# Three raw weight buffers, weight combinations made later, and an activation stash read straight into the operand

## The reference

```python
def swiglu(h, w1, w3, w2):
    return (jax.nn.silu(h @ w1) * (h @ w3)) @ w2
...
    x = x + 0.5 * swiglu(rmsnorm(x, ffn1_norm[l]), ffn1_w1[l], ffn1_w3[l], ffn1_w2[l])
    h = rmsnorm(x, mix_norm[l])
    proj = h @ w_in[l]                                   # (B,S,IN_W)
    ...
    o = jnp.concatenate([o_fox, o_moba, o_mem], axis=1)  # (B,16,S,Dh)
    ...
    x = x + o @ w_out[l]
    x = x + 0.5 * swiglu(rmsnorm(x, ffn2_norm[l]), ffn2_w1[l], ffn2_w3[l], ffn2_w2[l])
```

## Time and profile before

| | |
|---|---|
| runs | 4636.07, 4637.81, 4639.07 us |
| the profiled execution | 4634.58 us; its slowest core's span 4633.0 us |
| spans of cores 0 to 7 | 4633.0, 4618.8, 4598.5, 4592.8, 4629.0, 4617.3, 4626.0, 4613.5 us |
| TensorE (PE) busy, core 0 | 4378.5 us, 95% |
| VectorE (DVE), ScalarE (ACT) | 3280.9 us, 71%; 1508.3 us, 33% |
| DMA queues | software (GpSimd's) 43.0%, hardware (SyncE's) 26.3% of 16 engines |
| granted TensorE clock | 0.990 on average |

### The profile page before, as it was taken

The page is one execution under the profiler, slowest core; times in us unless marked ns, Lnnn a source line. Parts: engine busy times, 40 slices in busy tenths (PEclk is TensorE's granted clock), DMA queues, the critical chain, the costliest instruction groups (busy, mean ns, idle before and its releaser), DMA issues.

```text
span 4633.0 us, 66912 instructions; the slowest of 8 cores (4592.8 to 4633.0 us)
## 1 busy us (share of the span) xinstructions
PE 4378.5 (95%) x20213; PEld 1992.2 (43%) x20624; DVE 3280.9 (71%) x5577; ACT 1508.3 (33%) x2688; POOL 199.2 (4%) x357
## 2 busy tenths in 40 slices
PE   6998999999999998989999999799999999999999
PEld 2443444444444443444444444344444444444444
DVE  6675778766767876765566777667777887767776
ACT  2323212123121223556559872132221212122121
POOL 0000000000000000000010000000000000000000
PEclk9999999999999999999999999899999999999999
DMA  5788698876949887523357537877869785776845
GB/s 143 118 189 185 136 205 189 194 176 139 206 89 201 198 178 192 140 59 83 78 133 142 120 99 217 211 165 150 168 122 212 176 240 115 157 155 121 195 92 182
DMA packets 229027, 726.35 MB, mean 157 GB/s; under 512 B 25584, under 2 KB 53336, under 8 KB 186176
## 3 DMA queue, kind: packets, MB, share of 16 engines
q0 software_dynamic: 49312, 349.20, 43.0%
q1 hardware_dynamic: 179360, 372.84, 26.3%
HBM read 884.30 MB, written 167.94 MB: 227 GB/s over the span
## 4 chain that ended last, share of the span: by engine, by line
PE 75%; DMA 11%; DVE 5%; ACT 4%; issue 3%; SPq 1%; DVEq 0%; ACTq 0%; POOLq 0%; POOL 0%
PE ps L375 75%; DMA out<-xst 2%; DMA wraw<-wu 2%; ACT hrb L372 2%; DMA xst<-out 2%; DMA wraw<-wd 2%; DMA out<-yst 1%; DVE wcmb L350 1%; SPq L127 1%; DMA xst<-xr 1%; DMA wraw<-wob 1%; DMA bt<-Hs 1%; DVE acc L350 1%; ACT t_e L367 1%; DVE t_c L350 1%
## 5 line engine op out<-in xcount | busy, mean ns | idle before, releaser
L375 PE MATMUL ps<-XA,wcmb 128*128 128x512 bf16 x7998 | 1809.3, 380 | 27.9 <-ACT t_e L367 10.4
L375 PEld LDWEIGHTS ps<-XA,wcmb 128*128 128x128 bf16 x8160 | 797.1, 98 | 992.4 <-issue 52.2
L350 DVE TENSOR_TENSOR wcmb<-wraw 128x1024 bf16<-128x1024 bf16 (+1 forms) x1585 | 1013.4, 671 | 240.7 <-DMA wraw<-wd 125.0
L375 PE MATMUL ps<-XB,wcmb 128*128 128x512 bf16 x4554 | 1035.4, 381 | 62.7 <-DVE t_c L350 40.0
L367 ACT COPY t_e<-ps 128x512 f32<-128x512 f32 x984 | 570.8, 583 | 1280.2 <-PE ps L375 1059.0
L375 PE MATMUL ps<-XA,wraw 128*128 128x512 bf16 x3191 | 754.5, 383 | 42.4 <-DVE XA L350 38.5
L375 PEld LDWEIGHTS ps<-XB,wcmb 128*128 128x128 bf16 x4640 | 451.4, 98 | 618.4 <-issue 91.0
L375 PEld LDWEIGHTS ps<-XA,wraw 128*128 128x128 bf16 x3264 | 320.0, 98 | 432.1 <-issue 60.8
L350 DVE TENSOR_TENSOR t_c<-ps,t_e 128x512 f32<-128x512 f32 x328 | 225.6, 688 | 334.0 <-PE ps L375 313.6
L375 PE MATMUL ps<-XB,wraw 128*128 128x512 bf16 x1810 | 426.7, 381 | 21.9 <-DVE XB L350 18.3
L350 DVE TENSOR_TENSOR t_c<-t_e,ps 128x512 f32<-128x512 f32 x328 | 224.2, 683 | 191.6 <-PE ps L375 183.6
(11 more groups left out here) (155 smaller groups left out, 2756.8 us busy)
## 6 DMA issues: line engine op xcount, KB each, us to landing
wraw<-wu POOLq DMA_DIRECT2D x176, 1024.0 KB, 9.9
wraw<-wd POOLq DMA_DIRECT2D x64, 896.0 KB, 12.9
out<-yst SPq DMA_DIRECT2D x224, 256.0 KB, 13.2
out<-xst SPq DMA_DIRECT2D x208, 256.0 KB, 16.7
yst<-out SPq DMA_DIRECT2D x192, 256.0 KB, 14.2
xst<-out SPq DMA_DIRECT2D x48, 1024.0 KB, 8.7
xst<-out SPq DMA_DIRECT2D x176, 256.0 KB, 14.2
wraw<-wp POOLq DMA_DIRECT2D x29, 1024.0 KB, 8.9
```

The costliest lines, as they stand in the source:

```text
L350: return op(eng, lambda e: e.tensor_tensor(out=o_, in0=a, in1=b, op=alu), R=[a, b], W=[o_])
L375: return op("pe", lambda e: e.matmul(o_, l, r, start=start, stop=stop, skip_group_check=skip), R=[l, r], W=[o_])
```

## The change

- **Buffers.** `wraw` gets a third buffer (t % 3); `wcmb` becomes a single one. Quad t now issues the load of tile t+3. One tile of the output projection (`hold`) is not loaded ahead, because its buffer serves attention; `outproj` loads it at its start. `startup` loads three tiles.
- **Combinations.** Quad t makes c[0], c[1], c[2] of tile t+1 late (before `d22`, before `d11`, behind `d11`), into places whose last readers, products 5, 1 and 2, are past. c[3] and c[4] are made in quad t+1 itself, behind products 3 and 4.
- **`fresh`.** The first quad of each of the 12 down sections does its products in the order 5, 3, 4, 2, 1, 6, 7.
- **Rings.** `xstats` uses all four residual buffers and loads three steps ahead; `xstash` uses three and loads two ahead. `xbuild` stays at two.
- **The stash.** `Hs` is laid out so that a partition's four chunks of one form stand in one 4-KB row. `xfetch` issues all of it in its steps 0 and 1 (four 1-MB DMAs) straight into forms 1, 4, 5, 6 of `XA`, and makes the five forms in place, two chunks an instruction: 20 instead of 40 instructions, from step 2 on.

```diff
-        wraw = [sb("wraw%d" % i, [128, 4096], BF16, (112 + 8 * i) * KB) for i in range(2)]
-        wcmb = [sb("wcmb%d" % i, [128, 5120], BF16, (128 + 10 * i) * KB) for i in range(2)]
+        wraw = [sb("wraw%d" % i, [128, 4096], BF16, (112 + 8 * i) * KB) for i in range(3)]
+        wcmb = sb("wcmb", [128, 5120], BF16, 136 * KB)
...
+        pend, hold = {}, [-1]
...
-            prep = w_prep(t + 1) if last_use else []
+            own = pend.pop(t, [])
+            nxt = w_prep(t + 1) if last_use else []
...
+            if fresh:
+                prod(5, b11, True)
             prod(3, b22, True)
             acopy(e3, b22)
-            pr(2)
+            pr(own)
             prod(4, Z, True)
             acopy(e4, Z)
-            if last_use:
-                w_load(t + 2)
-            pr(1)
-            prod(5, b11, True)
+            while own:
+                pr(own)
+            if last_use and t + 3 != hold[0]:
+                w_load(t + 3)
+            if not fresh:
+                prod(5, b11, True)
             tt(c12, e3, b11, ALU.subtract)
             a12(c12)
+            if fresh:
+                prod(2, b21, True)
+                tt(c21, b21, e4, ALU.add)
             prod(1, Z, False)
             acopy(e14, Z)
-            pr(1)
             bgstep()
-            prod(2, b21, True)
-            tt(c21, b21, e4, ALU.add)
+            if not fresh:
+                prod(2, b21, True)
+                tt(c21, b21, e4, ALU.add)
             tt(w, e14, c21, ALU.subtract)
             a21(c21)
-            pr(1)
+            pr(nxt)
             prod(6, b22, False)
             tt(d22, b22, w, ALU.add)
             a22(d22)
+            pr(nxt)
             prod(7, b11, False)
             tt(d11, b11, e14, ALU.add)
+            pr(nxt)
             a11(d11)
+            if nxt:
+                pend[t + 1] = nxt
...
-        def xchunks(src, tag, tp, use):
+        def xchunks(src, tag, tp, use, ring=RING2):
+            la = len(ring) - 1
...
                     if c < 8:
-                        xst_load(src, tag, tp, c)
-                    if c:
-                        use(c - 1, xst[(c - 1) % 2])
+                        xst_load(src, tag, tp, c, ring)
+                    if c >= la:
+                        use(c - la, ring[(c - la) % len(ring)][1])
...
-                dma("sp", Hs[tp, c], flat(h), "hs%d" % (c % 2), W=[("H", tp, c)])
-            return xchunks(src, tag, tp, use)
+                dma("sp", Hs[tp, c // 4, :, :, c % 4, :], h[:, :, :], "hs%d" % (c % 2), W=[("H", tp, c)])
+            return xchunks(src, tag, tp, use, RING3)
...
         def xfetch(X, tp):
-            def load(c):
-                dma("sp", X[:, 1:5:3, c, :], Hs[tp, c, :, 0:1024].rearrange("p (a b) -> p a b", a=2), "hx%d" % (c % 2), R=[("H", tp, c)],
-                    W=[X[:, 1, c, :], X[:, 4, c, :]])
-                dma("sp", flat(bt[c % 2]), Hs[tp, c, :, 1024:2048], "hy%d" % (c % 2), R=[("H", tp, c)])
...
+            def load(h):
+                for n, (lo, hi, st) in enumerate(((1, 5, 3), (5, 7, 1))):
+                    o_ = X[:, lo:hi:st, 4 * h:4 * h + 4, :].rearrange("p a b c -> p a (b c)")
+                    dma("sp", o_, Hs[tp, h, :, 2 * n:2 * n + 2, :, :].rearrange("p a b c -> p a (b c)"), "hx%d%d" % (h, n),
+                        R=[("H", tp, 4 * h + i) for i in range(4)], W=[X[:, i, 4 * h:4 * h + 4, :] for i in range(lo, hi, st)])
+
+            def ops(c):
+                v = lambda i: X[:, i, c:c + 2, :]
+                return [(2, 5, 4, ALU.add), (3, 6, 1, ALU.subtract), (0, 1, 4, ALU.subtract), (5, 1, 5, ALU.add), (6, 6, 4, ALU.subtract)], v
...
-                    if k == 0:
-                        load(0)
+                    if k < 2:
+                        load(k)
                     else:
-                        comb(k - 1)
...
+                        for _ in range(4 if k < 4 else 3):
+                            todo.pop(0)()
...
-                dquads_sum(tl, XB, tp, xr if f == 0 and b == 0 else out, yst + xst, stats and b == 2)
+                dquads_sum(tl, XB, tp, xr if f == 0 and b == 0 else out, yst + xst, stats and b == 2, fresh=True)
...
+            w_load(ot[0][2])
             dquads_sum(ot[0], XA, 0, out, yst + xst, True)
```

More of the change, by code:

```diff
@@ L390, in w_load @@
                 R = list(R) + tag
[L391 removed]
+                dma("pool", wraw[t % 3][:, 0:4 * nk * 128], src, "wraw%d" % (t % 3), R=list(R))
         def w_views(t):
             nk = tasks[t][1]
[L395 to L396 removed]
+            raw = wraw[t % 3][:, 0:4 * nk * 128].rearrange("p (q c n) -> p q c n", q=4, c=nk)
+            cmb = wcmb[:, 0:5 * nk * 128].rearrange("p (q c n) -> p q c n", q=5, c=nk)
             return raw, cmb
@@ L402, in w_prep @@
             n = tasks[t][1] * 128
-            A11, A12, A21, A22 = [wraw[t % 2][:, i * n:(i + 1) * n] for i in range(4)]
-            c = [wcmb[t % 2][:, i * n:(i + 1) * n] for i in range(5)]
+            A11, A12, A21, A22 = [wraw[t % 3][:, i * n:(i + 1) * n] for i in range(4)]
+            c = [wcmb[:, i * n:(i + 1) * n] for i in range(5)]
             return [lambda: tt(c[0], A11, A12, ALU.add),
@@ L413, in build, with quad @@
         qcount = [0]
-        def quad(t, X, d22, d11, a12, a21, a22, a11, last_use=True, o12=None, o21=None):
+        pend, hold = {}, [-1]
+        def quad(t, X, d22, d11, a12, a21, a22, a11, last_use=True, o12=None, o21=None, fresh=False):
             raw, cmb = w_views(t)
@@ L510, in rt, with xst_load @@
             return [("R", tp, c, i) for i in range(4)]
-        def xst_load(src, tag, tp, c):
-            dma("sp", flat(xst[c % 2]), src[tp, c], "xst%d" % (c % 2), R=rt(tp, c) if tag == "R" else [])
+        RING2, RING3, RING4 = [(2, xst[0]), (3, xst[1])], [(2, xst[0]), (3, xst[1]), (1, yst[1])], [(2, xst[0]), (3, xst[1]), (1, yst[1]), (0, yst[0])]
+        def xst_load(src, tag, tp, c, ring):
+            i, b = ring[c % len(ring)]
+            dma("sp", flat(b), src[tp, c], "xst%d" % i, R=rt(tp, c) if tag == "R" else [])
         def conv():
@@ L550, in use @@
                     defer(6, stats_finish)
-            return xchunks(src, tag, tp, use)
+            return xchunks(src, tag, tp, use, RING4)
         noop = lambda: None
@@ L616, in build @@
                 ot = [[add(wo[dp], 8) if h == 0 and dp < 2 else add(wob[dp], 8, [("wo", dp)]) for dp in range(8)] for h in range(2)]
+                hold[0] = ot[0][2]
             for tp in range(2):
@@ L799, in dquads_mix, with dquads_sum @@
                     R=[y[:, 0, :], y[:, 3, :]] + t03, W=t03, add=True)
-        def dquads_sum(tl, X, tp, src, ring, stats):
+        def dquads_sum(tl, X, tp, src, ring, stats, fresh=False):
             n = len(ring)
@@ L823, in acc @@
                     return g
-                quad(tl[dp], X, tmp["s12"][:, :], tmp["s11"][:, :], acc(1), acc(2), acc(3), acc(0))
+                quad(tl[dp], X, tmp["s12"][:, :], tmp["s11"][:, :], acc(1), acc(2), acc(3), acc(0), fresh=fresh and dp == 0)
             if stats:
```

31 lines of the change are left out of this document (12 added, 19 removed).

## The result

The changed kernel takes 4604.52 us (median of 9 runs, lowest 4593.62) where the kernel before took 4637.81; the ratio of its runs to those of the kernel before is 0.9934, 95% interval 0.991 to 0.9958. (In some executions the granted clock of one die is lower, 0.94 in one of these nine; ratios here leave such executions out.) The forecast was 4562. So of about 76 us some 31 came.

A forecast was written before the change was run, and what follows sets the result against it. TensorE was busy 4378.5 of 4633.0 us, leaving 254.5 us idle, mostly in DMA-full stretches. Terms 11 + 9 + 16 + 24 + 12 + 9 = 81 off 4634.6 gave 4553.6; with 3.2 and 5 added, 4562 us, range 4522 to 4605.

The forecast's parts named there:

- `fresh`, 11 us: First quads of 12 down sections: TensorE stands 0.8 instead of 1.7 us for form 2; 11 us, bounds 5 to 18.
- `xstats`, 9 us: First `xstats` chunk: a lead of three quads ends TensorE's 9.3 us of idle time; 9 us, bounds 0 to 10.
- Stash, 24 us: Block-2 down sections of the first feed-forward: earlier issue lands the stash in time; 24 us, bounds 10 to 31.
- Third weight buffer, 16 us: Eight nk = 7 down sections: weight waits go, residual waits are late next; 16 us of 36.2, bounds 5 to 30.
- The rule that I weighed: Stash stretch: DMA engines alternate between queues, so the 4-MB bunch cannot delay weights; their deeper queue takes residual turns.
- The short leash: Single `wcmb`: TensorE waits when VectorE is over 3.5 us behind; 1.5 us in some 72 quads, 4670 us, chance 0.04.
- The two rivals: Late residual loads take the weights' place, 4622 us, chance 0.05; late combinations make TensorE wait, 4670 us, chance 0.04.
- Output projection, 12 us: Second half: the 8.29 us weight wait goes, the residual chunk's wait stays; 12 us of 30.5, bounds 3 to 20.
- Clock, 9 us: Four stretches with lowered granted clock: it rises as stalls go; 9 us, bounds 0 to 15.
- My rival of the full DMA engines: Long stretches with DMA shares of 0.91 to 0.98: earlier issue moves no byte away; 52 us gained, 4591, chance 0.20.
- My sign of being wrong: Whole kernel: the forecast is wrong if TensorE's idle time stays above 210 us.
- The two signs for the rivals: VectorE's `xst`/`yst` waits past 60 us show late residual loads; any TensorE wait on `wcmb` shows late combinations.

The follow-up runs named there:

- weights-undone kernel: Changed kernel with two raw and two combination buffers, loads two tiles ahead and combinations where they were before; the rest stays as changed: ratio 0.9877 to the kernel before.

## Why the prediction was right and wrong

**`fresh`, 11 us: right.** The wait on `XB` is 5.1 us for 18.3, the step at the border 0.58 for 1.55, and 18.7 us more stand there without it. VectorE's chain came out as predicted, except that the combinations around `d11` cost TensorE less: it stands 0.6 us, not 0.8. Without late combinations nothing is left of the wait, which was my upper bound of 18.

**`xstats`, 9 us: right.** 26.5 to 14.7, with about 1 us of `fresh` in it, and the weights-undone kernel has it too (16.4).

**Stash, 24 us: right in mechanism, too large.** The two sections lose 17.6 us (16.8 in the second trace of the changed kernel, 21.7 with the weights' part undone). I put the first half 24 us behind its issue, and its last DMA lands after just that, and the second half on the ground by the end of quad 3, before quad 4 asks for it. In half 0 this pair held SyncE's queue for 10.16 us, landed 33 and 42 us after its issue, and at 884.24 VectorE had stood 13.97 us for it. "It fits narrowly" was the sentence; on this core it did not. The longest such wait is 0.5 to 14.0 us on the eight cores. The stash's stores land a median 8.8 us after issue, for 5.0 before, but 5.2 with the weights' part undone, so their short rows, for which I had named a microsecond or two, are not what delays them.

**Third weight buffer, 16 us: the step that failed.** "So the weight waits on VectorE go. What is late next is the residual ... whose lead does not change. ... I let half of the rest go." The first half is exact: not one of VectorE's weight waits is left. But I took the 30.2 us for the residual as what would stay, and counted the rest as gain. VectorE, no longer held up by weights, arrives earlier at its additions, and the loads for them land 2 to 3 us later against their quad than before: 59 us of waits became 126. Of the sections' time nothing was left for this part: down sections and those behind them 63.1 before, 62.7 after, 51.6 with the weights' part undone, where only `fresh` acts. So the weights' part did not gain 16 us there but lost about 11. Two runs divide it. With the weights two tiles ahead the same sections have 58.8, with three ahead and earlier combinations 49.4: the late place of the combinations is what costs, and the third tile buys nothing. Seventeen products from issue to use were more than needed; ten products are 15 us against a landing of 12.9.

What the stretch does respond to is bytes. Length times DMA share over the eight windows of the earlier trace rows is 812 us of 832.3 before, 804 of 820.4 with the change, 804 of 821.8 with the weights' part undone. Halving the bytes of four of the eight sections' weights brought their residual down sooner and gave 12 to 18 us, with every lead as it was.

The rule that I weighed is borne out in part. DVE's waits in these sections sit on the residual alone, and in the block-2 down sections, with the 4-MB bunch, weight tiles land as soon as before (median 13.2 us after issue, 13.8 before): both are what I had drawn from the Trainium skill, DMA: Bandwidth & Descriptors, Arbitration (each engine goes round between the queues it has work for). That the deeper weight queue takes turns from the residual, which I had drawn from it too, no run shows; with the queue as deep as before the residual is as late.

**The short leash came with it.** I priced it as a lag that VectorE always has, and rejected it since the fullest section idles 0.5 us. The arithmetic held: 3.5 us of allowance, no loss below. But single waits of 4 to 8 us for the residual exceed it, and each then reaches TensorE through c[1] or c[2], as at 610.22: 62.7 us in 21 waits. Before, the same lateness was in `t_c` (48.8). The two rivals were written as separate cases; they are one chain, the first feeding the second. Earlier combinations without overlap take 10.8 us off the up sections and 2.5 off the down sections.

**Output projection, 12 us: failed, with the sign wrong.** I named a room of 11.5 us at a share of 0.91, and still gave all of it. The first half, where I had put no change, has 11.4 for 8.3, in both traces of the changed kernel; it is back at 8.3 to 8.6 wherever the combinations are not late, so they made it. The second half has 39.3 and 35.9 for 34.0. Its cause is open: it stays at 38.7 with earlier combinations and is 34.5 with the weights' part undone. Without the accumulating stores it falls by 18.6 to 22.0 us, through their bytes or through what waits for them.

**Clock, 9 us: failed.** The granted clock is 0.95 to 0.93, 0.96 to 0.98 and 0.90 to 0.90 in the long stretches of the earlier trace rows; only around the `xstats` chunk it rose, 0.83 to 1.00, where the stall went. It followed the idle time, and the idle time stayed.

**Not forecast.** The other sections lose 16.0 us. The first up section of each of the four halves goes from 39.8 to 37.2, 15.1 to 11.9, 18.8 to 14.1 and 4.0 to 2.7; some 4 of these 11.8 us are `fresh`, which I had counted. The first nine quads of the projections go from 22.2 to 18.0. They have 17.3 with the weights two ahead, 26.2 with earlier combinations and 22.8 with the weights' part undone, so here the late combinations help, not the third buffer. The middle 22 quads of the projections lost 2.9.

The sum: forecast 81 for the span, measured 35.2 on the mean of the cores. (The slowest core is 13 us over the mean, 17 before, so the allowance of 5 for another core was no error of weight.) Missing are 22 in the nk = 7 sections and behind them (16 + 7 x 0.9 forecast, 0.4 found), 20 in the output projection (12 forecast, 8.4 lost), 9 of clock, 6 of stash and 3 in the projections; some 15 in `xstats`, the first up sections, the first nine quads and attention come off. My rival of the full DMA engines, 4591, was nearer to the 4604 than the forecast.

My sign of being wrong did not appear: TensorE's idle time is 186.9 us, under the 210 I had set. It was set against 254.5 us, of which 13 to 26 were work without a record. The two signs for the rivals did appear, `xst` and `yst` at 87.6 us and `wcmb` at 62.7.

What stays open: how much faster the kernel is with the weights' part undone, since the intervals overlap; why the middle of the projections loses 2.9 us with the change (88.5 with earlier combinations, 85.2 with the weights' part undone); what in the accumulating stores costs the output projection its time.

## What to carry to other kernels

Before pricing a longer lead, ask what the engine that waits will stand for next, and how much later that lands; here 223 us of waits for weights became 67 more for the residual and no shorter section. Multiply the DMA share of the stretch by its length as well: where that is 97% of the time, as here, expect little from a deeper buffer; half the weights' bytes gave what it did not. Try a deeper buffer and a later use apart: here the later use alone ended the waits. A combination (or any step that TensorE needs soon) that moves behind a step which can wait for a DMA inherits that wait; look for what stands ahead of the new place in program order, not only at how long it takes. And check the count of matmul records before idle time is read off a page: 411 missing ones made 13 to 26 us.

## What the hardware did that I had not expected

- Large work on the software queue comes with late small transfers on the hardware queue: with one 896-KB conversion a quad, stores of `KTs` kept VectorE up to 9.9 us, and with conversions in attention a head's load of `aq` kept TensorE up to 39.2 us. The same kernel without the conversions has neither wait.
- Issue itself can block: the second stash pair held SyncE's queue for 10.16 us, and everything behind it; the stash's loads landed 10.7 (shortest) to 42.3 us (longest) after their issue on this core.
- The 512-KB accumulating stores are dear: without eight of them, and what waits for them, a stretch of 126 us is 18.6 to 22.0 us shorter.
